# Twenty residual loads of a second output product: eight spread over SyncE's weight loads, twelve begun by ScalarE

## The chip, the cores and the metric

The kernel runs on one core of a Trainium2 chip. The metric is the device time of one execution in microseconds (us). The core's engines are TensorE (PE, matrix products), VectorE (DVE), ScalarE (ACT), GpSimd (POOL) and SyncE (SP), which here only begins transfers. Each works through its own instruction list in order and waits on semaphores for the others. Transfers between the main memory (HBM) and the on-chip memory (SBUF) are begun by SyncE, ScalarE or GpSimd and carried by 16 DMA engines.

## The reference

One layer over 128 context tokens and 512 noisy tokens, 1024 features each, all in float32:

```
x = x + 0.5 * gt1 * swiglu(norm(x) * (1 + sc1) + sh1, w_ffn1_in, w_ffn1_out)
x = x + gt2 * mixer(norm(x) * (1 + sc2) + sh2)          # convolution and gated DeltaNet heads
x = x + 0.5 * gt3 * swiglu(norm(x) * (1 + sc3) + sh3, w_ffn2_in, w_ffn2_out)
y = norm(x) * norm_final
...
def _swiglu(h, w_in, w_out):
    a, b = jnp.split(h @ w_in, 2, axis=-1)
    return (jax.nn.silu(a) * b) @ w_out
```

The change lies in the last product, `(silu(a) * b) @ w_ffn2_out` with 2816 hidden features, and in the residual `x` that is added to it.

## The kernel before

Float32 values are split into a high half (`_hi`, rounded to the format that TensorE takes at speed) and a low half (`_lo`, the rest), and each product is made of three matmuls: high by high, high by low, low by high. ScalarE makes the high halves, VectorE the low ones.

Until the second SwiGLU's input product the activations lie features by tokens. The second output product turns this round: the hidden activations `g` are the stationary operand and a row of weights is the moving one, 128 hidden features (partitions) by 512 output columns, so that the result lies tokens by features. The weights come as 84 such rows, numbered p. One row passes a line of stations:

- SyncE (`load_out_rows`, line 666) loads row p into `w_row`, a ring of eight buffers, from the weights `in_w_ffn_out` or from `d_ws`, a table of sums of weight blocks that GpSimd has written to HBM earlier. From row 8 on it waits until row p - 8 has its low half.
- ScalarE (`out_hi`, line 1884) makes `ring_hi` of it, a ring of four, and waits for TensorE to be done with row p - 4.
- VectorE (`out_lo`, line 2600) makes `ring_lo`.
- TensorE (`stripe`, line 1543) multiplies, in matmuls of 128x128 by 128x512.

Between the weight rows ScalarE and VectorE also make the halves of `g` (`g_hi`, line 1874, and `g_lo`, line 2593; tiles `gs_hi` and, in the plain rows, `gp_hi`).

The rows come in this order. Rows 0 to 31 are eight groups of four (`four`), six matmuls a row. Rows 32 to 55 are eight groups of three (`left`). Rows 56 to 61 are the six plain rows of the left half of the columns (`p_plain(0, r)`), for each of which TensorE makes five products of three matmuls. Rows 62 to 77 are eight groups of two (`right`), rows 78 to 83 the plain rows of the right half.

The residual comes back in this stage. Earlier VectorE has turned `x` in blocks of 32x32 into `xb`, and SyncE has stored it features by tokens in the HBM table `d_xb`. A residual load brings 32 tokens (partitions) by 1024 features into `yo`, as 32x32 runs of 32 numbers, 128 bytes each; 20 such loads, four for each of the five token tiles, bring all 640 tokens. VectorE waits for all of them at once, and for the two gate broadcasts `gb`, after it has made the low half of row 65:

```
for k in range(1, NH):
    for j in range(2):
        out_lo(p_right(k, j))
    if k == 1:
        dve.wait_ge(in_rows, 16 * (T // 32 + 2))
    if k > 1 and k - 2 < NC:
        residual_rows(0, k - 2)
```

`residual_rows` multiplies a result by the gate (`moved`) and adds it to `yo`. After the last row ScalarE and VectorE sum squares, normalise, and SyncE stores the outputs.

The kernel before has all 20 residual loads in SyncE's list, inside the loop over the weight rows (`load_out_rows`).

Of the kernel before, what the change touches and what calls it, by code (L numbers as in the profile page):

```python
# [36 lines left out]
P = 128  # L37
D = 1024
KD = D // P
TP, TS = 128, 512  # L40
T = TP + TS
TH = T // 2
NC = T // P
# [39 lines left out]
def p_four(k, j):  # L83
    return 4 * k + j
# [6 lines left out]
def p_right(k, j):  # L91
    return 7 * NH + NPL + 2 * k + j

def p_plain(c, r):
    return (7 + 2 * c) * NH + NPL * c + r

def w_block(p):

    if p < 4 * NH:
        k, j = divmod(p, 4)
        return ((k, 0, None), (k, 0, 1), (k, 0, 0), (k, 0, 2))[j]
    if p < 7 * NH:
        k, j = divmod(p - 4 * NH, 3)
        return ((k, 0, None), (NH + k, 0, None), (k, 0, 3))[j]
    if p < p_right(0, 0):
        return p - 5 * NH, 0, None
    n = p - p_right(0, 0)
    return (n // 2 + NH * (n % 2) if n < 2 * NH else n), 1, None  # L110
# [51 lines left out]
def hybrid_layer(nc, x_prompt, x_sample, state_f, state_b, c, c_ctx, w_ada, b_ada, norm1, w1i, w1o, norm_mix,  # L162
# [3 lines left out]
    with ctx:  # L166
# [3 lines left out]
        def sb(name, shape, dt, at=None):  # L170
            size = int(np.prod(shape[1:])) * (2 if dt == BF16 else 4)
            if at is None:
                at = place["at"]
                place["at"] += (size + 31) // 32 * 32
            return nc.alloc_sbuf_tensor_at(name, shape, dt, offset=at)
# [160 lines left out]
        def view(t, dims):  # L336

            return bass.AP(tensor=t.tensor, offset=t.offset, ap=dims)
# [13 lines left out]
        yo = sb("yo", [P, NC, D], F32, at=at_h + 12 * KB)  # L352
# [31 lines left out]
        d_xb = nc.dram_tensor("d_xb", [KD, P, T], F32).ap()  # L384
# [102 lines left out]
        xt_rdy, st_rows, in_rows = (sem(n) for n in ("xt_rdy", "st_rows", "in_rows"))  # L487
# [32 lines left out]
        def operand(p):  # L520

            return w_raws[p % 8], raw_in(p)

        PIECES = ((0, 0, TP, 0, 0), (0, TP, TH, 1, TP), (1, 0, TH, 1, TH))

# [49 lines left out]
        def _(sp):  # L576
# [75 lines left out]
            def load_out_rows():  # L652

                sp.wait_ge(st_rows, 16 * (GROUPS_DN + 2 + KD + 2))
                for i in range(2):
                    sp.wait_ge(ws_in[i], WS_IN)
                for n in range(R_ALL):
                    if n == 4:
                        sp.wait_ge(pr_done, LAST + 5)
                    if n == 6:  # L660
                        sp.wait_ge(*c12_rdy(SE[1] - 1))
                    if n >= 8:
                        sp.wait_ge(*lo_of(n - 8))
                    row, c, made = w_block(n)
                    src = w_out_v[1][:, row, OW * c:OW * c + OW] if made is None else d_ws[made, row]
                    sp.dma_start(w_raws[n % 8][:, :], src).then_inc(fr_in[n % 8], 16)
                    if n == 10:
                        sp.wait_ge(pr_done, 7 * SE[1])
                        sp.wait_ge(op_rdy, 7 * SE[1])
                        for j in range(2):  # L670
                            sp.dma_start(gb[:, j, :], d_gate[j:j + 1, :].to_broadcast([P, D])).then_inc(in_rows, 16)
                    if n >= 12 and n % 2 == 0 and (n - 12) // 2 < NC:
                        t = (n - 12) // 2
                        for b in range(4):
                            sp.dma_start(yo[32 * b:32 * b + 32, t, :].rearrange("p (c j) -> p c j", j=32),
                                         view(d_xb[0, 0, P * t + 32 * b:], [[T, 32], [32 * T, D // 32], [1, 32]])
                                         ).then_inc(in_rows, 16)
                    if n == p_right(3, 1):
                        sp.dma_start(nf_b[:, :], norm_f.rearrange("(a f) -> a f", a=1).to_broadcast([P, D])
                                     ).then_inc(nf_in, 16)  # L680
# [13 lines left out]
            def load_pairs(f):  # L694

                sp.wait_ge(mm_done, U_OUT[f])
                load_pair(f, S0[f] + 1, 1, pair_cols(NP[f] + 1))
                r0 = S0[f] // 2 + 1
                if f == 1:
                    for k in range(KD):  # L700
                        s = 2 * r0 + k
                        sp.wait_ge(op_rdy, 7 * s - 8)
                        load_pair(f, s, k % 2, pair_cols(NP[f] - S0[f] + s))
                        store_turned(k)
                    r0 += KD // 2
                with sp.Fori(r0, SE[f] // 2) as r:
                    for q in range(2):
                        sp.wait_ge(op_rdy, 14 * r + (7 * q - 8))
                        load_pair(f, None, q, lambda b: bass.ds(2 * P * r + (P * (NP[f] - S0[f] + q) + b * FF), P))
                sp.wait_ge(op_rdy, 7 * (SE[f] - 2) + 6)  # L710
                if f == 0:
                    load_out_columns(U_OUT[f], w_out_v[f])
                else:
                    load_out_rows()
# [938 lines left out]
        def _(act):  # L1653
# [195 lines left out]
            def g_hi(i):  # L1849

                if i < 2 * NH:
                    k = i // 2
                    act.wait_ge(pr_done, LAST + (2, 2, 3, 3, 3, 4, 4, 6)[k])
                    act.wait_ge(*s_made(k))
                    dst = gs_hi[:, k, 2 * (i % 2):2 * (i % 2) + 2, :].rearrange("p a t -> p (a t)")
                    src = g32[:, k, P:5 * P] if i % 2 == 0 else xs[:, k, :]
                elif i < 4 * NH:
                    k = i // 2 - NH
                    act.wait_ge(*mm_of(p_four(k, 3)))
                    if i % 2 == 0:  # L1860
                        dst, src = gs_hi[:, k, 0:2, :].rearrange("p a t -> p (a t)"), g32[:, NH + k, P:5 * P]
                    else:
                        dst = gs_hi[:, k, 3, :].rearrange("p (a t) -> p a t", a=2)
                        src = g32[:, k:k + NH + 1:NH, 0:P]
                elif i < 4 * NH + NPL:
                    r = i - 4 * NH
                    act.wait_ge(*mm_of(p_four(NH - 1, 3)))
                    act.wait_ge(*g_made(1, 2 * NH + r))
                    dst, src = gp_hi[:, r, :], g32[:, 2 * NH + r, :]
                else:  # L1870
                    b = i - 4 * NH - NPL
                    act.wait_ge(ps_rdy, PS + (8 if b == 0 else 15))
                    dst, src = gs_hi[:, 4 * b:4 * b + 4, 2, :], s4[b][:, :, :]
                nc.scalar.activation(dst, src, ACT.Copy).then_inc(gh_rdy, 1)

            def out_hi(p):

                src, ready = operand(p)
                act.wait_ge(*ready)
                if p > 3:  # L1880
                    act.wait_ge(*mm_of(p - 4))
                else:
                    act.wait_ge(pr_done, LAST + (1, 1, 6, 6)[p])
                nc.scalar.activation(ring_hi[p % 4][:, :], src[:, :], ACT.Copy).then_inc(fo_hi, 1)  # L1884
# [403 lines left out]
            for k in range(NH - 1):  # L2288
                p = p_four(k + 1, 0)
# [23 lines left out]
            for r in range(NPL):  # L2313
                g_hi(4 * NH + r)
                out_hi(p_plain(0, r))
            for b in range(2):
                out_hi(p_right(0, b))
                g_hi(4 * NH + NPL + b)
# [20 lines left out]
        def _(dve):  # L2339
# [423 lines left out]
            def residual(m, j, done, a_slot, n):  # L2763

                dve.wait_ge(mm_done, done)
                if j == 0:
                    dve.wait_ge(gain_rdy, 5 if m else 4)
                for bnk, b0, b1, i, t0 in PIECES:
                    last = nc.vector.scalar_tensor_tensor(
# [791 lines left out]
```

## Time and profile before

| | |
|---|---|
| median of 3 runs | 1294.96 us (1290.78 to 1295.73) |
| the profiled execution's own time | 1295.59 us |
| its span, first to last instruction | 1293.7 us |
| TensorE busy | 1264.2 us (98%) |
| VectorE, ScalarE, GpSimd busy | 983.6, 588.1, 141.5 us |
| second output product, row 0 to the first store | 1136.69 to 1282.72 us |

All times within the profiled execution count from the start of its span. The profile gives busy time, idle time and what ended it (the releaser) by engine, line and tile. TensorE's matmuls overlap in a pipeline: of two matmuls in a row, the distance between their starts is what one costs.

### The profile page before, as it was taken

How to read it: one execution, taken by the hardware profiler on the slowest of the kernel's cores; microseconds unless marked ns; L12 is line 12 of the kernel's file. 1: busy time of each engine (PE TensorE's matmuls, PEld its weight loads, DVE VectorE, ACT ScalarE, POOL GpSimd, SP SyncE). 2: the span in 40 equal slices, each digit the busy share in tenths (PEclk: the TensorE clock that was granted, in tenths of full speed). 3: DMA queues.
4: the chain of work that ended last, by engine and by line, in shares of the span. 5: the costliest groups of instructions: out<-in, count | busy, mean ns of one | idle time of the engine just before them, and what ended most of it. 6: DMA issues, size and time to landing. Idle time of an engine off the chain costs nothing.

```text
span 1293.7 us, 23360 instructions
## 1 busy us (share of the span) xinstructions
PE 1264.2 (98%) x8861; PEld 1211.0 (94%) x8861; DVE 983.6 (76%) x1646; ACT 588.1 (45%) x1002; POOL 141.5 (11%) x145
## 2 busy tenths in 40 slices
PE   8999999999999999999999999999999999988997
PEld 7889999999999999999999899999999999976886
DVE  5668877787887864666899867647988898867767
ACT  6514543345532225664333553436544343456643
POOL 0000222222000000003323663000000000000000
PEclk9999999999999999999999999999999999999999
DMA  9871767666576735348873552242243423287642
GB/s 371 295 270 31 190 153 191 156 163 166 163 215 194 220 107 142 99 119 190 260 211 64 154 149 83 66 88 60 66 128 96 143 71 97 65 212 233 191 139 90
DMA packets 250615, 197.31 MB, mean 153 GB/s; under 512 B 48321, under 2 KB 211622, under 8 KB 249254
## 3 DMA queue, kind: packets, MB, share of 16 engines
q1 hardware_dynamic: 241076, 176.00, 45.6%
q0 software_dynamic: 7840, 19.40, 7.5%
q8 instruction: 53, 0.87, 0.3%
q10 hardware_dynamic: 1618, 0.81, 0.2%
q14 instruction: 28, 0.23, 0.1%
HBM read 181.58 MB, written 36.61 MB: 169 GB/s over the span
## 4 chain that ended last, share of the span: by engine, by line
PE 74%; DVE 9%; DMA 6%; ACT 4%; issue 3%; POOL 2%; another core or an unknown queue 0%; SPq 0%; POOLq 0%; DVEq 0%; ACTq 0%
PE ps L1123 32%; PE ps L930 24%; PE ps L1543 8%; PE ps L1500 3%; DMA d_ex<-d_gc 2%; DMA w_row<-d_ws 2%; PE ps L1053 1%; DVE w_lo L2344 1%; DMA w_raw<-in_w_ffn_in 1%; PE ps L1486 1%; DVE cv L2831 1%; ACT w_hi L1659 1%; DVE sub_tmp L2951 1%; DVE pn L2413 1%; PE ps L998 1%
## 5 line engine op out<-in xcount | busy, mean ns | idle before, releaser
L1659 ACT ACTIVATE w_hi<-w_raw 128x1024 fp32r<-128x1024 f32 (+1 forms) x79 | 81.8, 1036 | 205.9 <-PE ps L930 163.8
L930 PE MATMUL ps<-h_hi,w_hi 128*128 128x320 f32 x736 | 171.9, 315 | 2.8 <-DVE w_lo L2344 2.7
L930 PE MATMUL ps<-h_lo,w_hi 128*128 128x320 f32 x736 | 169.5, 311 | 0.0
L930 PE MATMUL ps<-h_hi,w_lo 128*128 128x320 f32 x736 | 169.2, 311 | 0.0
L930 PEld LDWEIGHTS ps<-h_hi,w_hi 128*128 128x128 f32 x736 | 123.6, 189 | 7.5 <-issue 7.2
L2344 DVE TENSOR_TENSOR w_lo<-w_raw,w_hi 128x1024 fp32r<-128x1024 f32 (+1 forms) x79 | 100.0, 1267 | 37.2 <-ACT w_hi L1659 35.1
L1123 PE MATMUL ps<-T_hi,S_hi 128*128 128x320 f32 x408 | 126.0, 309 | 0.0
L1123 PE MATMUL ps<-T_hi,S_lo 128*128 128x320 f32 x408 | 126.0, 309 | 0.0
L1123 PE MATMUL ps<-T_lo,S_hi 128*128 128x320 f32 x408 | 125.9, 309 | 0.0
L930 PEld LDWEIGHTS ps<-h_hi,w_lo 128*128 128x128 f32 x736 | 124.6, 189 | 0.0
L930 PEld LDWEIGHTS ps<-h_lo,w_hi 128*128 128x128 f32 x736 | 124.3, 189 | 0.0
L2752 DVE SCALAR_TENSOR_TENSOR cw_acc<-cw_raw,silu_c,cw_acc 128x1024 f32<-128x1024 f32 x70 | 86.1, 1279 | 8.4 <-DMA cw_raw<-in_w_ada 5.7
L2600 DVE TENSOR_TENSOR ring_lo<-w_row,ring_hi 128x512 fp32r<-128x512 f32 x84 | 57.1, 688 | 42.6 <-ACT ring_hi L1884 41.3
L1123 PE MATMUL ps<-B_hi,A_hi 128*128 128x320 f32 x264 | 81.5, 309 | 0.5 <-issue 0.5
L1123 PE MATMUL ps<-B_lo,A_hi 128*128 128x320 f32 x264 | 81.4, 308 | 0.0
L1123 PE MATMUL ps<-B_hi,A_lo 128*128 128x320 f32 x264 | 81.4, 308 | 0.0
L1884 ACT ACTIVATE ring_hi<-w_row 128x512 fp32r<-128x512 f32 x84 | 52.4, 628 | 63.6 <-PE ps L1543 45.4
L930 PE MATMUL ps<-g_hi,w_hi 128*128 128x320 f32 x352 | 80.8, 311 | 0.2 <-DVE w_lo L2344 0.2
L930 PE MATMUL ps<-g_lo,w_hi 128*128 128x320 f32 x352 | 80.2, 309 | 0.0
L930 PE MATMUL ps<-g_hi,w_lo 128*128 128x320 f32 x352 | 80.2, 309 | 0.0
L1836 ACT ACTIVATE sa<-ps 128x320 f32<-128x320 f32 x34 | 14.9, 438 | 135.9 <-PE ps L1123 135.9
L1123 PEld LDWEIGHTS ps<-T_lo,S_hi 128*128 128x128 f32 x408 | 76.6, 188 | 0.0
(429 smaller groups left out, 3194.0 us busy)
## 6 DMA issues: line engine op xcount, KB each, us to landing
w_raw<-in_w_ffn_in SPq DMA_DIRECT2D x50, 512.0 KB, 4.8
cw_raw<-in_w_ada SPq DMA_DIRECT2D x40, 512.0 KB, 4.4
w_more<-in_w_ffn_in SPq DMA_DIRECT2D x34, 512.0 KB, 5.1
ada_w<-in_w_ada SPq DMA_DIRECT2D x16, 1024.0 KB, 9.0
w_raw<-in_w_mix_in SPq DMA_DIRECT2D x28, 512.0 KB, 4.4
w_row<-in_w_ffn_out SPq DMA_DIRECT2D x52, 256.0 KB, 3.0
d_ws<-in_w_ffn_out POOLq DMA_DIRECT2D x48, 256.0 KB, 5.3
w_row<-d_ws SPq DMA_DIRECT2D x32, 256.0 KB, 3.7
```

Source lines behind the costliest of these rows:

```text
L930: last = pe.matmul(to[a_slot][b], w, m[:, k0 + k, part[b]], start=start and k == 0 and n == 0, stop=stop and k == kt - 1 and n == 2)
L998: last = pe.matmul(adap[32 * g:32 * g + 32, 0:512], ccol[:, k, :], ada_w[:, n % ADA, g * 512:(g + 1) * 512], start=k == 0, stop=k == KD - 1)
L1053: pe.matmul(accw[s][b], w, m[:, k, PARTW[b]], start=k == 0 and n == 0, stop=k == KD - 1 and n == 2)
L1123: last = pe.matmul(to, a, m[:, k, :], start=not again and k == 0 and n == 0, stop=k == 3 and n == 2, skip_group_check=again)
L1500: last = pe.matmul(acc[s][b], w, m[:, k % 4, PART[b]], start=k == 0 and n == 0, stop=k == KD - 1 and n == 2)
L1543: last = pe.matmul(ps[bank][:, 0:f1 - f0], g, w, start=start and n == 0, stop=stop and n == 2, skip_group_check=True)
L1659: nc.scalar.activation(w_hi[:, slot, 0:kt * P], w_raw[:, slot, 0:kt * P], ACT.Copy).then_inc(hi_ready, 1)
L1836: nc.scalar.activation(c11, X, ACT.Silu).then_inc(act_ev, 1)
L1884: nc.scalar.activation(ring_hi[p % 4][:, :], src[:, :], ACT.Copy).then_inc(fo_hi, 1)
L2344: nc.vector.tensor_tensor(w_lo[:, slot, 0:kt * P], w_raw[:, slot, 0:kt * P], w_hi[:, slot, 0:kt * P].bitcast(F32), ALU.subtract).then_inc( ...
L2600: nc.vector.tensor_tensor(ring_lo[p % 4][:, :], operand(p)[0][:, :], ring_hi[p % 4][:, :].bitcast(F32), ALU.subtract).then_inc(fo_rdy, 1)
L2752: nc.vector.scalar_tensor_tensor(out=to[:, i, :], in0=raw_at(n)[:, :], scalar=silu_c[:, k, i:i + 1], in1=to[:, i, :], op0=ALU.mult, op1=AL ...
```

## The change

The four residual loads of a token tile stood together behind each of the weight loads 12, 14, 16, 18 and 20. Now a function `turned_rows(eng, i)` begins the i-th of the 20 loads on an engine of choice. SyncE begins loads 0 to 7, one behind each of the weight loads 12, 14, ..., 26. ScalarE begins loads 8 to 19, two behind the high half of each plain row 56 to 61. VectorE's wait for all 20 stays where it is.

```diff
+        def turned_rows(eng, i):
+
+            t, b = divmod(i, 4)
+            eng.dma_start(yo[32 * b:32 * b + 32, t, :].rearrange("p (c j) -> p c j", j=32),
+                          view(d_xb[0, 0, P * t + 32 * b:], [[T, 32], [32 * T, D // 32], [1, 32]])).then_inc(in_rows, 16)
+
...
-                    if n >= 12 and n % 2 == 0 and (n - 12) // 2 < NC:
-                        t = (n - 12) // 2
-                        for b in range(4):
-                            sp.dma_start(yo[32 * b:32 * b + 32, t, :].rearrange("p (c j) -> p c j", j=32),
-                                         view(d_xb[0, 0, P * t + 32 * b:], [[T, 32], [32 * T, D // 32], [1, 32]])
-                                         ).then_inc(in_rows, 16)
+                    if n >= 12 and n % 2 == 0 and (n - 12) // 2 < 4 * 2:
+                        turned_rows(sp, (n - 12) // 2)
...
             for r in range(NPL):
                 g_hi(4 * NH + r)
                 out_hi(p_plain(0, r))
+                for i in range(2):
+                    turned_rows(act, 8 + 2 * r + i)
```

In SyncE's list, from the gate broadcasts on, weight loads (`w_row_...`, one number for each of the eight ring buffers) and residual loads (`yo`) stood so before:

```order
L671 DMA gb<-d_gate 128x1024 x2
L666 DMA w_row_196<-d_ws 128x512
L666 DMA w_row_197<-in_w_ffn_out 128x512
L675 DMA yo<-d_xb 32x32x32 x4
L666 DMA w_row_198<-d_ws 128x512
L666 DMA w_row_199<-d_ws 128x512
L675 DMA yo<-d_xb 32x32x32 x4
L666 DMA w_row_200<-d_ws 128x512
L666 DMA w_row_193<-in_w_ffn_out 128x512
L675 DMA yo<-d_xb 32x32x32 x4
```

The same place of SyncE's list in the changed kernel, where line 527 is `turned_rows`:

```order
L677 DMA gb<-d_gate 128x1024 x2
L672 DMA w_row_196<-d_ws 128x512
L672 DMA w_row_197<-in_w_ffn_out 128x512
L527 DMA yo<-d_xb 32x32x32
L672 DMA w_row_198<-d_ws 128x512
L672 DMA w_row_199<-d_ws 128x512
L527 DMA yo<-d_xb 32x32x32
L672 DMA w_row_200<-d_ws 128x512
L672 DMA w_row_193<-in_w_ffn_out 128x512
L527 DMA yo<-d_xb 32x32x32
```

Three of four residual loads have gone from between the pairs of weight loads; the weight loads keep their order, and three more pairs have a residual load behind them than before.

In ScalarE's list, at the first plain rows, the high halves of `g` (`gp_hi`) and of the weight rows (`ring_hi`) stood so before:

```order
L1874 ACTIVATE gp_hi<-g_223 128x640
L1884 ACTIVATE ring_hi_201<-w_row_193 128x512
L1874 ACTIVATE gp_hi<-g_223 128x640
L1884 ACTIVATE ring_hi_202<-w_row_194 128x512
L1874 ACTIVATE gp_hi<-g_223 128x640
L1884 ACTIVATE ring_hi_203<-w_row_195 128x512
```

The same place of ScalarE's list in the changed kernel:

```order
L1876 ACTIVATE gp_hi<-g_223 128x640
L1886 ACTIVATE ring_hi_201<-w_row_193 128x512
L527 DMA yo<-d_xb 32x32x32 x2
L1876 ACTIVATE gp_hi<-g_223 128x640
L1886 ACTIVATE ring_hi_202<-w_row_194 128x512
L527 DMA yo<-d_xb 32x32x32 x2
L1876 ACTIVATE gp_hi<-g_223 128x640
L1886 ACTIVATE ring_hi_203<-w_row_195 128x512
L527 DMA yo<-d_xb 32x32x32 x2
```

Two residual loads now stand between the high half of a plain row and the halves behind it, six times over.

## Rows read from the trace of the kernel before

**Rows 1.** The page's busy us, share of the span, and instructions of TensorE.

```profile
PE 1264.2 (98%) x8861; PEld 1211.0 (94%) x8861; DVE 983.6 (76%) x1646; ACT 588.1 (45%) x1002; POOL 141.5 (11%) x145
```

**Rows 2.** Who waited for whom, 1110 to 1293: us in total, times, longest.

```profile
ACT ring_hi L1884 <- DMA w_row<-d_ws: 15.6, 8, 3.5
...
PE ps L1543 <- DVE ring_lo L2600: 7.5, 7, 1.8
```

**Rows 3.** TensorE's timeline: start, duration (us), line, operation, [idle before it].

```profile
1136.69 0.40 PE L1543 MATMUL ps<-ring_hi,gs_hi 128*128 128x512 f32 x1
...
1153.21 0.39 PE L1543 MATMUL ps<-ring_hi,gs_hi 128*128 128x512 f32 x1
...
1173.91 0.51 PE L1543 MATMUL ps<-ring_hi,gs_hi 128*128 128x512 f32 x1 [1.70 <-DVE ring_lo L2600]
```

**Rows 4.** Second output's line by stretch: length, busy us (count) on PE and PEld, PEclk, DMA.

```profile
1136.60:1173.80 37.20, 30.29 (x126) 23.14 (x126) 1.00 0.93 231
1136.60:1153.10 16.50, 16.41 (x72) 13.57 (x73) 1.00 0.83 242
```

**Rows 5.** SyncE's timeline: start, us to issue the run, transfers in it.

```profile
1142.06 7.51 SPq L675 DMA_DIRECT2D yo<-d_xb  x4
...
1150.69 3.91 SPq L675 DMA_DIRECT2D yo<-d_xb  x4
...
1155.83 3.55 SPq L675 DMA_DIRECT2D yo<-d_xb  x4
...
1160.60 3.63 SPq L675 DMA_DIRECT2D yo<-d_xb  x4
...
1165.40 3.55 SPq L675 DMA_DIRECT2D yo<-d_xb  x4
```

**Rows 6.** Busy us by engine in stretches, then PEclk, DMA share, GB/s.

```profile
1155.00:1160.00 5.00, 3.39 (x14) 2.50 (x15) 2.33 (x4) 1.73 (x4) 0.00 (x0) 1.00 1.08 221
1175.00:1180.00 5.00, 5.00 (x24) 4.11 (x23) 4.69 (x9) 3.79 (x8) 0.00 (x0) 1.00 1.00 375
1210.00:1220.00 10.00, 10.00 (x46) 8.29 (x45) 6.43 (x11) 6.26 (x12) 0.00 (x0) 1.00 0.65 199
1220.00:1230.00 10.00, 10.00 (x45) 8.13 (x44) 6.91 (x11) 5.45 (x9) 0.00 (x0) 1.00 0.50 150
1230.00:1240.00 10.00, 10.00 (x45) 8.04 (x44) 4.34 (x5) 3.79 (x5) 0.00 (x0) 1.00 0.36 121
```

**Rows 7.** The chain that ended last, 1100 to 1294: start, us, what.

```profile
1140.62 7.62 DMA w_row<-d_ws
...
1195.06 82.31 PE ps L1543 x357
```

**Rows 8.** The residual's tile, 1138 to 1172: ns to issue one, us to landing.

```profile
L675 SPq DMA_DIRECT2D yo<-d_xb x20: 303/566/3592, 1142.1 to 1168.6; - x20
...
DMA to landing us min/median/max: 2.7/4.0/7.8
```

**Rows 9.** ScalarE's timeline at the first plain rows (56, 57, 61).

```profile
1219.25 0.63 ACT L1884 ACTIVATE ring_hi<-w_row 128x512 fp32r<-128x512 f32 x1
...
1220.42 0.61 ACT L1884 ACTIVATE ring_hi<-w_row 128x512 fp32r<-128x512 f32 x1
...
1230.35 0.63 ACT L1884 ACTIVATE ring_hi<-w_row 128x512 fp32r<-128x512 f32 x1 [2.24 <-PE ps L1543]
```

**Rows 10.** TensorE's timeline where rows 56 and 57 begin.

```profile
1223.08 0.40 PE L1543 MATMUL ps<-ring_hi,gp_hi 128*128 128x512 f32 x1
...
1226.59 0.40 PE L1543 MATMUL ps<-ring_hi,gp_hi 128*128 128x512 f32 x1
```

**Rows 11.** VectorE's timeline at rows 64, and 65 with 66.

```profile
1241.51 0.69 DVE L2600 TENSOR_TENSOR ring_lo<-w_row,ring_hi 128x512 fp32r<-128x512 f32 x1 [1.32 <-ACT ring_hi L1884]
1245.01 1.46 DVE L2600 TENSOR_TENSOR ring_lo<-w_row,ring_hi 128x512 fp32r<-128x512 f32 x2 [2.81 <-ACT ring_hi L1884]
```

**Rows 12.** A transfer begun by ScalarE earlier in the program.

```profile
690.01 0.62 ACTq L2070 DMA_DIRECT2D d_sel<-sub_x  x1
```

## Prediction

> **What bounds the kernel now.** I read the busy shares first. TensorE is busy for 98% of a 1293.7 us span [rows 1], so only a stretch in which it stands still has time to give, or one that makes it stand still. The change touches the second output stage alone (from 1136.7 us on), so I read next who waits for whom there. TensorE's matmuls stood idle 7.5 us in 7 waits for `ring_lo`, VectorE's low half of a weight row, and ScalarE's `ring_hi` waited 15.6 us for 8 weight loads from `d_ws` [rows 2]. So weight rows land late, and through ScalarE and VectorE TensorE waits for them.
>
> Third, the size of the loss, from starts of matmuls instead of idle times, since a matmul after a stall also runs slower at first. Row 0 starts at 1136.69; 72 matmuls (12 rows of six) later it is 1153.21, so one takes (1153.21 - 1136.69) / 72 = 0.2294 us and a row 1.376 us [rows 3]. Ahead of the matmul at 1173.91 stand 126 matmuls [rows 4], or 21 rows. They should take 126 x 0.2294 = 28.9 us; they took 37.2. **TensorE loses 8.3 us here.** It falls ahead of rows 13 to 21, since the first 72 matmuls show no idle time beyond 0.1 us (16.41 of 16.50 us busy) [rows 4].
>
> Fourth, why they are late. SyncE's queue shows four residual loads in one piece after every second weight load: 7.51 us for the first four, then 3.91, 3.55 and 3.63 [rows 5]. From block to block it is 5.14, 4.77 and then 4.80 us to the fifth at 1165.40 [rows 5], for two weight rows that TensorE uses up in 2.75. The 16 DMA engines are full then: share 1.08 at 221 GB/s, where weights alone get 375 GB/s at share 1.00 [rows 6]. A weight load of 262,144 bytes so costs 0.70 us of all engines, and a residual load (4.79 - 2 x 0.70) / 4 = **0.85 us**, for half the bytes. Residuals hold up weights by filling the engines in front of them; that SyncE is held while it issues is the same backlog seen from the queue.
>
> **The change, part by part.** No matmul, byte or VectorE instruction is added or removed. What moves is 20 residual loads.
>
> *Eight stay on SyncE, one behind each second weight load.* Each pair of rows then asks for 1.40 + 0.85 = 2.25 us of the engines, under the 2.75 us in which TensorE uses it. So the supply is faster than the demand, if row 13 is in time. The load of row 11, issued at 1140.62, landed 7.62 us later, at 1148.2 [rows 7], behind the two gate broadcasts. Behind it now come row 12 (0.70), one residual (0.85) and row 13 (0.70): 1150.5. TensorE wants row 13 at 1136.69 + 13 x 1.376 = 1154.6, and the two halves take 0.63 and 0.69 ahead of that [rows 9, 11], so it must land by 1153.2. There are 2.7 us in hand, and each pair adds 0.5. So I count the full 8.3 us as gained. The lower bound takes the residual at its dearest, 7.51 / 4 = 1.88 us [rows 5]: a pair then asks 3.28 us, 0.53 too much, over eight pairs 4.2 us. Less the 2.7 in hand, 1.5 is lost and 6.8 gained; with nothing in hand, 4.1. I take 0.85 because the last two intervals between blocks give it, and the one before gives 0.94; the first block stood behind the gate broadcasts.
>
> *Twelve go to ScalarE, two behind each `ring_hi` of the six plain rows.* ScalarE is in order, so each pair holds up the next `gp_hi` and `ring_hi`, VectorE's `ring_lo` behind them, and then TensorE. ScalarE's `ring_hi` of row 56 starts at 1219.25 and that of row 57 at 1220.42: 1.17 us a row without the loads [rows 9]. TensorE begins row 56 at 1223.08 and row 57 at 1226.59: 3.51 us a row [rows 10]. With an issue of x us, the low half of row 56 + r is ready 2.51 + r (2.34 - 2x) us ahead of TensorE (2.51 is 1223.08 less 1219.25, 0.63 and 0.69; 2.34 is 3.51 less 1.17). For row 62, the first behind all twelve, that is 16.55 - 12x: no stall up to x = 1.38. ScalarE has issued no residual so far. Its nearest row, a small store, took 0.62 us [rows 12]; on SyncE a residual took 0.30 at least, 0.57 in the middle, 3.59 at most [rows 8], and 0.89 (3.55 / 4) in a full queue [rows 5]. I take at most 0.89, because the plain rows have free engines: **nothing** on the path. The upper end is 3.59: row 62 would be 26.5 us late.
>
> *The engines there.* Twelve loads take 12 x 0.85 = 10.2 us. From 1210 to 1240 the DMA share is 0.65, 0.50 and 0.36 [rows 6], so 3.5 + 5.0 + 6.4 = 14.9 us are free. Weight loads run eight rows, some 28 us, ahead. Cost nothing; without that cover, up to 10.2 us.
>
> *VectorE's wait for all residuals moves from long satisfied to near.* It stands behind the low half of row 65, whose pair with row 66 begins at 1245.01, so at 1245.6 [rows 11]. Queued behind it are the low halves of rows 66 on and the first residual sums. ScalarE reaches row 61 at 1230.35, held by TensorE and not by its loads [rows 9]; two issues of 0.89 end at 1232.8, and the slowest landing was 7.8 us [rows 8]: 1240.6. That is 5.0 us in time; the likely landing of 4.0 us leaves 8.8.
>
> *Behind the stage.* TensorE's next piece on the chain runs 82.31 us, from 1195.06 [rows 7], with VectorE's and ScalarE's tail behind it. Nothing there waits for a transfer that the stalls had given time to, so 8.3 us go through. 
>
> **The rivals.** *Half stays* (gain 4.1, 1290.9): residuals cost 1.88 us each and row 13 has nothing in hand. For it speaks the first block; against it the three that follow. *The stalls are the weights' own* (no change, 1295): every long wait is for `d_ws` rows, which might land late whatever stands before them. Against it: at 1175 the same rows come at 375 GB/s and TensorE is busy 5.00 of 5.00 us [rows 6].
>
> *The work only moves* (1296.9 at worst): the engines' work is conserved, and the twelve loads hold up weights among the plain rows for all of their 10.2 us, which eats the 8.3. Against it stand the 14.9 us free and the eight rows of lead. The Trainium skill speaks for this rival ("DMA: Bandwidth & Descriptors", "Issuing engines are not separate DMA queues"): loads begun by ScalarE and SyncE run on the same 16 engines, and a second issuer saves only its sequencer's time. By that rule the move to ScalarE gives nothing by itself; the trace agrees in that the engines, not SyncE, are full, and what is left as a gain is the later hour.
>
> *ScalarE becomes the wait* (slower): at x over 1.38 us row 62 is late. The loss is 12x - 16.55, so it decides at x = 2.07, where 8.3 us are eaten; at 3.59 the sum is 1294.96 - 8.3 + 26.5 = 1313.2. For it: SyncE did take 3.59 once. Against: that was behind the gate broadcasts, on full engines.
>
> **How the numbers follow.** Chances: forecast 0.66, half stays 0.09, weights' own 0.10, work only moves 0.07, ScalarE 0.08. A measurement of this kernel tells about 0.5%, 6.5 us. The forecast's own spread (6.8 to 8.3, and some noise of a median of runs that lie 5 us apart) falls beyond that in nine of ten: 0.60 faster, and 0.01 from the other cases. ScalarE's case is over 6.5 us slower from x = 2.61 on, most of it as its rows are either near 0.9 or near 3.6: 0.06. The rest, 0.33, is the same. The range goes from 1284 (the forecast less 2.7 of noise) to 1292.5, which takes in half stays and leaves out no change and slower: about 0.8. The forecast alone: 1284 to 1289.5.
>
> **What would show it.** In the changed profile, matmul 126 of the stage should start some 29 us after row 0, not 37; `ring_hi`'s waits for `d_ws` should be nearly gone; two weight rows and a residual should pass SyncE every 2.75 us; ScalarE should issue each residual in under 1 us; `ring_lo` of row 62 should not be waited for; VectorE should go from row 65's low half to row 66's without a wait for a DMA. Wrong would be: stalls of rows 13 to 20 that stay, an issue above 1.4 us on ScalarE, or a wait for `yo` at row 65.

## The result, and the profile of the changed kernel

The changed kernel takes 1287.94 us (median of 19 runs, 1283.78 to 1291.91), the kernel before 1296.75 (19 runs beside them, 1290.78 to 1302.33). The ratio is 0.9933, with a 95% interval of 0.9920 to 0.9946: 8.7 us less (1296.75 x 0.0067). The forecast was 8.3 us less, taken from a median of three runs of the kernel before, 1294.96; beside the changed kernel its median was 1.8 us higher.

Of the two profiled executions the spans are 1293.7 and 1286.7 us, 7.0 apart. That is less than the gain of the stage itself, because row 0 of the second output product starts at 1138.13 instead of 1136.69: the work ahead of the stage took 1.4 us longer in this execution. Over all profiles below row 0 starts anywhere from 1133.82 to 1141.11, in no order that follows from the edits. So the stage is best measured from its own first matmul. From row 0 to the last matmul start of the line it took 1286.92 - 1136.69 = 150.23 us before and 1279.92 - 1138.13 = 141.79 us after: **8.44 us less**. The last matmul before, and after:

```profile
1286.92 0.28 PE L1543 MATMUL ps<-ring_lo,gp_hi 128*128 128x256 f32 x1
```

```profile
1279.92 0.28 PE L1545 MATMUL ps<-ring_lo,gp_hi 128*128 128x256 f32 x1
```

From that start to the end of the span it is 6.8 us in both, and in every kernel below.

First, TensorE's timeline of the changed kernel (start, duration, line, operation) at row 0 and 126 matmuls later, and under it, as in [rows 4], the busy time and count of that line between the two:

```profile
1138.13 0.40 PE L1545 MATMUL ps<-ring_hi,gs_hi 128*128 128x512 f32 x1
...
1167.00 0.40 PE L1545 MATMUL ps<-ring_hi,gs_hi 128*128 128x512 f32 x1
```

```profile
1138.05:1166.95 28.90, 28.82 (x126) 23.79 (x127) 1.00 1.00 264
```

The same 126 matmuls now take 1167.00 - 1138.13 = 28.87 us instead of 37.22, and 28.82 of 28.90 us are busy. No stall is left ahead of rows 13 to 21. The waits of the whole stretch say the same (who waited for whom: us in total, times, longest; compare [rows 2]):

```profile
ACT ring_hi L1886 <- DMA w_row<-d_ws: 2.1, 1, 2.1
...
PE ps L1545 <- DVE ring_lo L2604: 0.6, 2, 0.4
```

ScalarE's waits for `d_ws` fell from 15.6 us to one of 2.1 us, TensorE's for `ring_lo` from 7.5 us to 0.6. The chain that ended last (start, us, what) has no transfer of a weight row in this stage any more:

```profile
1138.29 44.79 PE ps L1545 x195
...
1188.04 82.33 PE ps L1545 x357
```

Next SyncE's queue (start, us to issue, transfers), to be read beside [rows 5]: the first, the fourth and the last of its eight residual loads. Between the residual loads there are always two weight loads:

```profile
1143.50 0.74 SPq L527 DMA_DIRECT2D yo<-d_xb  x1
...
1154.47 0.43 SPq L527 DMA_DIRECT2D yo<-d_xb  x1
...
1163.37 0.43 SPq L527 DMA_DIRECT2D yo<-d_xb  x1
```

From the fourth to the eighth it is (1163.37 - 1154.47) / 4 = 2.23 us for two weight loads and a residual, while SyncE fills its ring of eight faster than TensorE empties it. The forecast's sum for the engines was 2.25.

ScalarE's part, at the plain rows: its activations and, marked ACTq, its issues of residual loads:

```profile
1212.25 0.63 ACT L1886 ACTIVATE ring_hi<-w_row 128x512 fp32r<-128x512 f32 x1
1212.27 0.99 ACTq L527 DMA_DIRECT2D yo<-d_xb  x2
1213.36 0.74 ACT L1876 ACTIVATE gp_hi<-g 128x640 fp32r<-128x640 f32 x1 [0.47 <-PE ps L1545]
1213.46 1.40 ACTq L527 DMA_DIRECT2D yo<-d_xb  x1
1214.00 0.62 ACT L1886 ACTIVATE ring_hi<-w_row 128x512 fp32r<-128x512 f32 x1
...
1224.21 0.62 ACT L1886 ACTIVATE ring_hi<-w_row 128x512 fp32r<-128x512 f32 x1
```

The twelve issues add up to 11.9 us, 0.99 each, more than the 0.89 that I took at most. Five of the twelve took 1.40 us or more, 1.52 the longest, and an issue above 1.4 us on ScalarE was one of the forecast's signs of being wrong; why it cost nothing stands below. The DMA engines were busier there than I had it (busy us by engine, PEclk, DMA share, GB/s; compare [rows 6]):

```profile
1155.00:1160.00 5.00, 5.00 (x24) 4.11 (x23) 4.45 (x8) 3.95 (x8) 0.00 (x0) 1.00 1.10 268
1210.00:1220.00 10.00, 10.00 (x45) 8.21 (x44) 6.47 (x10) 5.68 (x9) 0.00 (x0) 1.00 0.95 210
1220.00:1230.00 10.00, 10.00 (x44) 8.04 (x44) 4.86 (x7) 4.10 (x6) 0.00 (x0) 1.00 1.07 232
```

TensorE is busy in all of it. The last lines to check are VectorE's at rows 65 and 66, behind which its wait for all 20 residual loads stands, and the residual's own (ns to issue, us to landing):

```profile
1238.01 1.46 DVE L2604 TENSOR_TENSOR ring_lo<-w_row,ring_hi 128x512 fp32r<-128x512 f32 x2 [2.81 <-ACT ring_hi L1886]
```

```profile
L527 ACTq DMA_DIRECT2D yo<-d_xb x12: 367/1050/1515, 1212.3 to 1224.1; - x12
...
DMA to landing us min/median/max: 3.5/5.0/6.1
```

VectorE's two low halves run as one piece, so the wait between them cost nothing. The last issue began at 1224.1 and no landing took over 6.1 us: all residuals were there by 1230.2, 8.4 us before VectorE asked.

### The profile page after: what moved, and what is told of

The parts are those of the page before. It is cut to its first block, busy times and chain, and to the rows that moved or that the text cites. A ratio compares the mean times of both kernels' runs of the same rounds, so it can differ in the third digit from the quotient of the medians.

```text
span 1286.7 us, 23360 instructions
## 1 busy us (share of the span) xinstructions
PE 1262.6 (98%) x8861; PEld 1210.9 (94%) x8861; DVE 983.5 (76%) x1646; ACT 588.5 (46%) x1002; POOL 141.6 (11%) x145
## 4 chain that ended last, share of the span: by engine, by line
PE 77%; DVE 9%; DMA 4%; ACT 3%; issue 3%; POOL 2%; another core or an unknown queue 1%; SPq 0%; POOLq 0%; DVEq 0%; ACTq 0%
PE ps L1125 33%; PE ps L932 24%; PE ps L1545 10%; PE ps L1502 3%; DMA d_ex<-d_gc 2%; PE ps L1055 1%; DVE w_lo L2348 1%; DMA w_raw<-in_w_ffn_in 1%; PE ps L1488 1%; DVE cv L2835 1%; ACT w_hi L1661 1%; DVE sub_tmp L2955 1%; DVE pn L2417 1%; PE ps L1000 1%; POOL Rc L3472 1%
## 5 line engine op out<-in xcount | busy, mean ns | idle before, releaser
L1838 ACT ACTIVATE sa<-ps 128x320 f32<-128x320 f32 x34 | 14.9, 438 | 136.5 <-PE ps L1125 136.5
L1125 PEld LDWEIGHTS ps<-T_hi,S_hi 128*128 128x128 f32 x408 | 76.6, 188 | 0.0
```

The costliest lines, as they stand in the source:

```text
L1125: last = pe.matmul(to, a, m[:, k, :], start=not again and k == 0 and n == 0, stop=k == 3 and n == 2, skip_group_check=again)
L1838: nc.scalar.activation(c11, X, ACT.Silu).then_inc(act_ev, 1)
```

## The experiments

My theory is the one of the forecast: what delayed the weight rows was the time of the 16 DMA engines, 0.70 us for a weight load and 0.85 for a residual load, against 2.75 us in which TensorE uses two rows. Rivals: SyncE's list, held while it issues; the move to ScalarE; blocks of four as such; and rows of the table of sums that are late by themselves.

Every ratio below is to the kernel before, run beside the experiment: 1296.75 us beside the changed kernel, 1295.99 beside the next four, 1295.75 beside the last three, with 7 to 12 runs of each experiment. The stage counts from row 0 to the last matmul start, as above, in one profiled execution of each kernel; the four kernels near 141.8 us agree within 0.03 us.

| kernel | median, us | ratio (95%) | stage, us | against changed |
|---|---|---|---|---|
| before | 1296.75, 1295.99, 1295.75 | 1 | 150.23 | +8.44 |
| changed | 1287.94 | 0.9933 (0.9920 to 0.9946) | 141.79 | 0 |
| all 20 on SyncE | 1288.23 | 0.9941 (0.9922 to 0.9961) | 141.77 | -0.02 |
| blocks of four apart | 1287.21 | 0.9945 (0.9924 to 0.9966) | 141.76 | -0.03 |
| blocks among left rows | 1293.15 | 0.9972 (0.9953 to 0.9991) | 144.44 | +2.65 |
| ScalarE in one burst | 1294.15 | 0.9989 (0.9972 to 1.0005) | 148.84 | +7.05 |
| two a pair | 1293.74 | 0.9981 (0.9963 to 0.9998) | 147.30 | +5.51 |
| twelve by SyncE, same hour | 1287.82 | 0.9937 (0.9917 to 0.9957) | 141.77 | -0.02 |
| blocks by GpSimd | 1294.97 | 0.9997 (0.9978 to 1.0015) | 146.88 | +5.09 |

The ratios alone do not tell the burst and the blocks by GpSimd from the kernel before: their intervals include 1. Blocks among the left rows stand 5.8 us under before by the stage and 3.6 by the ratio; blocks by GpSimd 3.4 and 0.4. Behind the stage nothing differs, so the difference lies ahead of it or is noise; its cause stays open, and the readings below go by the stage.

**All 20 on SyncE.** Is it ScalarE that carries the gain? Here ScalarE begins none.

```diff
-                    if n >= 12 and n % 2 == 0 and (n - 12) // 2 < 4 * 2:
+                    if n >= 12 and n % 2 == 0 and (n - 12) // 2 < 4 * NC:
                         turned_rows(sp, (n - 12) // 2)
...
-                for i in range(2):
-                    turned_rows(act, 8 + 2 * r + i)
```

> All 20 residual loads on SyncE, one behind every second weight load (12, 14, ..., 50); ScalarE begins none. Theory (the 16 DMA engines: a pair of weight rows asks 1.40 + 0.85 = 2.25 us of them and TensorE takes 2.75): no stall, as fast as the changed kernel, 8 to 9 us under before (ratio 0.993). Rival (the move of twelve loads to ScalarE carries the gain): twelve twentieths of it are lost again, 3 to 4 us under before.

The stage takes 141.77 us, as in the changed kernel, and the ratios agree within their intervals. The move to ScalarE is not needed for the gain; the spreading is.

**Twelve by SyncE, at the same hour.** The twelve late loads stay at the hour of the plain rows, but SyncE begins them.

```diff
+                    if p_plain(0, 0) + 8 <= n < p_plain(0, NPL) + 8:
+                        for i in range(2):
+                            turned_rows(sp, 8 + 2 * (n - p_plain(0, 0) - 8) + i)
...
-                for i in range(2):
-                    turned_rows(act, 8 + 2 * r + i)
```

> As the changed kernel, but the twelve late loads are begun by SyncE, two behind each of the weight loads 64 to 69, which run at the hour of the plain rows. Theory (engines; it matters when a load runs, not who begins it): as the changed kernel within 1 us, 8 to 9 us under before. Rival (the second issuer matters): SyncE is held about 1 us a load and the weight rows come late, 2 us or more slower than the changed kernel.

Again 141.77 us. Who begins a load makes no difference here.

**Blocks by GpSimd.** The counter-test: the old hour and the old blocks, with SyncE's list free of residuals.

```diff
-                    if n >= 12 and n % 2 == 0 and (n - 12) // 2 < 4 * 2:
-                        turned_rows(sp, (n - 12) // 2)
...
-                for i in range(2):
-                    turned_rows(act, 8 + 2 * r + i)
...
-                    dve.wait_ge(in_rows, 16 * (T // 32 + 2))
+                    dve.wait_ge(in_rows, 16 * 2)
+                    dve.wait_ge(in_pool, 16 * (T // 32))
...
+            for t in range(NC):
+                pool.wait_ge(*lo_of(4 + 2 * t))
+                for b in range(4):
+                    turned_rows(pool, 4 * t + b, in_pool)
```

The residual loads count on a semaphore of their own here, `in_pool`, and VectorE waits for it at the old place.

> All 20 begun by GpSimd, in blocks of four let go when the low halves of rows 4, 6, 8, 10 and 12 are made, the hour of the blocks in the kernel before; SyncE begins weight rows only. Theory (engines full): weight rows late again ahead of rows 13 to 21, 5 us of stall or more, within 4 us of before, unless GpSimd itself spreads the loads out. Rival (SyncE's list was the trouble, not the engines): no stall, 8 to 9 us under before.

The stage lost 5.1 us to the changed kernel. TensorE's timeline shows the longest stalls, ahead of rows 13 to 15 ([idle before <- releaser]), and the windows the full engines (busy us by engine, PEclk, DMA share, GB/s):

```profile
1160.37 0.50 PE L1544 MATMUL ps<-ring_hi,gs_hi 128*128 128x512 f32 x1 [0.77 <-DVE ring_lo L2601]
...
1163.26 0.50 PE L1544 MATMUL ps<-ring_hi,gs_hi 128*128 128x512 f32 x1 [1.23 <-DVE ring_lo L2601]
...
1166.05 0.50 PE L1544 MATMUL ps<-ring_hi,gs_hi 128*128 128x512 f32 x1 [1.14 <-DVE ring_lo L2601]
```

```profile
1155.00:1160.00 5.00, 4.45 (x19) 3.02 (x17) 1.16 (x3) 1.67 (x3) 3.53 (x5) 1.00 1.06 237
1160.00:1165.00 5.00, 3.31 (x12) 2.10 (x12) 2.21 (x4) 1.62 (x4) 0.00 (x0) 1.00 1.04 230
```

SyncE was not held by a residual here, and the rows were late all the same. It began the load of row 13 at 1146.71, as the first of three, and ScalarE, which waited for it, took the row up at 1158.96:

```profile
1146.71 2.73 SPq L673 DMA_DIRECT2D w_row<-d_ws  x3
```

```profile
1158.96 0.63 ACT L1885 ACTIVATE ring_hi<-w_row 128x512 fp32r<-128x512 f32 x1 [1.79 <-DMA w_row<-d_ws]
```

That is 5.6 and 17.85 us after row 0. In the kernel with blocks among the left rows (below), where no residual is begun yet, SyncE begins the same load at 5.6 us too, and ScalarE takes the row up at 14.04 without waiting for it. So the rival of SyncE's list falls. The loss is smaller than before. GpSimd did not keep to blocks of four: it issued fifteen one behind the other, one every 0.78 us, stopped for 9.8 us and issued the last five:

```profile
1146.73 11.80 POOL L527 DMA_DIRECT2D yo<-d_xb  x15 [355.38 <-DVE ring_lo L2601]
1168.31 3.88 POOL L527 DMA_DIRECT2D yo<-d_xb  x5 [9.79 <-issue]
```

By the medians this kernel stands no better than before, though its stage is 3.4 us shorter; its row 0 started latest of all, at 1141.11, and whether GpSimd's wait or chance did that stays open.

**Blocks of four apart.** Is it the block?

```diff
-                    if n >= 12 and n % 2 == 0 and (n - 12) // 2 < 4 * 2:
-                        turned_rows(sp, (n - 12) // 2)
+                    if n >= 12 and (n - 12) % 8 == 0 and (n - 12) // 8 < NC:
+                        for i in range(4):
+                            turned_rows(sp, (n - 12) // 2 + i)
...
-                for i in range(2):
-                    turned_rows(act, 8 + 2 * r + i)
```

> The blocks of four of the kernel before, all on SyncE, but behind every eighth weight load (12, 20, ..., 44) instead of every second. Theory (engines, mean load): four pairs ask 4 x 1.40 + 3.4 = 9.0 us of 11.0, a block of 3.4 us meets 2.7 us in hand or more: at most 1 us of stall, 7.5 to 8.5 us under before. Rival (a block of four is in itself what stalls): five blocks at 2.0 us each, about as before (within 2 us).

The blocks did no harm: 141.76 us. ScalarE did wait for weight rows, and TensorE only for two short waits of 0.6 us together (us in total, times, longest):

```profile
ACT ring_hi L1887 <- DMA w_row<-d_ws: 10.0, 6, 2.8
...
PE ps L1546 <- DVE ring_lo L2603: 0.6, 2, 0.4
```

Ten us of waiting, up to 2.8 us at a time, stayed inside ScalarE's lead over TensorE. By the ratio this kernel is 7.1 us under before (4.4 to 9.8), by the stage 8.5, as forecast. A block does no harm if the lead covers it and the mean load leaves time to win the lead back.

**Blocks among the left rows.** Is it the table of sums? The five old blocks, at the old density, now among rows two thirds of which come from the weights themselves.

```diff
-                    if n >= 12 and n % 2 == 0 and (n - 12) // 2 < 4 * 2:
-                        turned_rows(sp, (n - 12) // 2)
+                    if n >= 34 and n % 2 == 0 and (n - 34) // 2 < NC:
+                        for i in range(4):
+                            turned_rows(sp, 2 * (n - 34) + i)
```

> The same five blocks of four behind every second weight load, but behind loads 34, 36, ..., 42, which are mostly rows of the weights themselves and only one in three from the table of sums; nothing but weights stands in rows 12 to 31. Theory (engines): five blocks ask 4.8 us for each pair that TensorE takes in 2.75, 10.2 us in all, less 3 to 7 us in hand since the gate broadcasts are long over: stalls of 3 to 7 us, 1.5 to 6 us under before. Rival (the rows of the table of sums are late by themselves): the stalls stay ahead of rows 13 to 21, about as before; rival (neither): no stall in the second place, 8 to 9 us under before.

Matmul 126 starts 28.87 us after row 0: with nothing but weights in rows 12 to 31, the stalls ahead of rows 13 to 21 are gone, although the rows from the table are the same. New stalls stand where the blocks are (TensorE's timeline):

```profile
1197.28 0.50 PE L1546 MATMUL ps<-ring_hi,gs_hi 128*128 128x512 f32 x1 [0.48 <-DVE ring_lo L2603]
...
1198.59 0.50 PE L1546 MATMUL ps<-ring_hi,gs_hi 128*128 128x512 f32 x1 [0.35 <-DVE ring_lo L2603]
...
1201.82 0.50 PE L1546 MATMUL ps<-ring_hi,gs_hi 128*128 128x512 f32 x1 [0.90 <-DVE ring_lo L2603]
```

So the rows from the table were not late by themselves. The price is 2.65 us, just under the 3 that I gave as the least: with the gate broadcasts out of the way there was more in hand. The load of row 34, the last one ahead of the blocks, landed 36.4 us after row 0, and TensorE takes that row at 47.3, 1.3 of which the two halves need: 9.6 us in hand, where I had 3 to 7.

**Two a pair.** Where is the threshold?

```diff
-                    if n >= 12 and n % 2 == 0 and (n - 12) // 2 < 4 * 2:
-                        turned_rows(sp, (n - 12) // 2)
+                    if n >= 12 and n % 2 == 0 and (n - 12) // 2 < 2 * NC:
+                        for i in range(2):
+                            turned_rows(sp, n - 12 + i)
```

> All 20 on SyncE, two behind each second weight load (12, 14, ..., 30). Theory (engines): a pair asks 1.40 + 1.70 = 3.10 us, 0.35 over TensorE's 2.75; ten pairs 3.5 us, less 2.7 in hand: a stall of about 1 us, 6 to 8.5 us under before. Rival (any residual load between the pairs costs in proportion to their number): two against four a pair, 4 us under before.

The rate was right and the loss was not. SyncE's queue, second and last pair:

```profile
1151.33 1.04 SPq L527 DMA_DIRECT2D yo<-d_xb  x2
...
1175.99 1.05 SPq L527 DMA_DIRECT2D yo<-d_xb  x2
```

Eight pairs apart, (1175.99 - 1151.33) / 8 = 3.08 us for SyncE to issue a pair of rows with its residuals, against 3.10 expected, and 0.33 over TensorE's 2.75. But the stage lost 5.51 us and not 1. Stalls ahead of rows 23 to 31 (the distances of starts beyond 0.23 us, added up) are 2.6 us. ScalarE's timeline at rows 13 and 31, which it takes up as soon as they have landed, tells why:

```profile
1152.61 0.63 ACT L1887 ACTIVATE ring_hi<-w_row 128x512 fp32r<-128x512 f32 x1 [1.16 <-DMA w_row<-d_ws]
...
1182.05 0.63 ACT L1887 ACTIVATE ring_hi<-w_row 128x512 fp32r<-128x512 f32 x1 [1.89 <-DMA w_row<-d_ws]
```

Over these nine pairs the rows landed (1182.05 - 1152.61) / 9 = 3.27 us apart, more than the 3.08 at which SyncE issued them and 0.52 over TensorE's 2.75: 4.7 us in all. Row 13 came 14.45 us after row 0, 2.1 us before it had to, and 4.7 less 2.1 is the 2.6 lost. More came behind row 31, where TensorE waited for `U`, a sum that VectorE makes after four low halves of `g` and one of a row, all queued behind row 31's low half:

```profile
1187.29 0.77 PE L1546 MATMUL ps<-ring_hi,gs_hi 128*128 128x512 f32 x1 [2.17 <-DVE U L3324]
1187.85 0.63 PE L1546 MATMUL ps<-ring_hi,g_lo 128*128 128x512 f32 x1
```

```profile
1186.00:1187.00 1.00, 0.00 (x0) 0.00 (x0) 1.00 (x2) 1.00 (x3) 0.00 (x0) 1.00 1.04 399
1187.00:1188.00 1.00, 0.71 (x2) 0.65 (x3) 1.00 (x3) 0.89 (x2) 0.00 (x0) 0.63 0.84 313
1188.00:1189.00 1.00, 1.00 (x4) 0.77 (x3) 1.00 (x3) 0.00 (x0) 0.00 (x0) 0.50 0.64 225
...
1191.00:1192.00 1.00, 1.00 (x6) 0.82 (x5) 1.00 (x3) 0.06 (x1) 0.00 (x0) 1.00 0.49 168
```

Together this is 2.6 + 2.3 + 1.7 = 6.6 us; the changed kernel has 1.1 us of waits for `ring_lo` at rows 32 and 35 that this one does not have, which leaves the 5.5. By the ratio the kernel stands 2.5 us under before, nearer the rival's 4 than the theory's 6 to 8.5. The rival falls all the same: one residual a pair, all 20 of them, cost nothing above, where in proportion it would have cost a quarter of the 8.4.

**ScalarE in one burst.** What does an issue cost where it does lie on the path?

```diff
-                for i in range(2):
-                    turned_rows(act, 8 + 2 * r + i)
+                if r == 0:
+                    for i in range(12):
+                        turned_rows(act, 8 + i)
```

> As the changed kernel, but ScalarE issues all twelve loads in one go behind the high half of row 56. Theory (ScalarE in order, 12 issues of about 1.0 us each against 2.51 + 2.34 = 4.85 us in hand at row 57): low half of row 57 is 5 to 7.5 us late, TensorE waits that long, 1 to 4 us under before. Rival (what ScalarE issues is hidden whatever its order): 8 to 9 us under before.

ScalarE's timeline and TensorE's behind it:

```profile
1211.75 0.63 ACT L1886 ACTIVATE ring_hi<-w_row 128x512 fp32r<-128x512 f32 x1
1211.77 10.33 ACTq L527 DMA_DIRECT2D yo<-d_xb  x12
1222.19 0.74 ACT L1876 ACTIVATE gp_hi<-g 128x640 fp32r<-128x640 f32 x1 [9.81 <-issue]
```

```profile
1218.85 0.40 PE L1545 MATMUL ps<-ring_lo,gp_hi 128*128 128x512 f32 x1
1224.44 0.80 PE L1545 MATMUL ps<-ring_hi,gp_hi 128*128 128x512 f32 x1 [5.19 <-DVE ring_lo L2605]
```

Twelve issues took 10.33 us, 0.86 each, which is the engines' price of a residual load: ScalarE was held at the pace at which the engines drained. With x = 0.86 the forecast's formula makes row 57 late by 12 x 0.86 - 4.85 = 5.5 us; TensorE started it 1224.44 - 1218.85 - 0.23 = 5.4 us late. ScalarE's issues are free in the changed kernel only because they are spread over six rows. The stage lost 7.05 us in all, 1.7 more than the wait: the granted clock fell to 0.50 during the wait and stood at 0.98 again in the stretch from 1228, 3.6 us after TensorE had gone on at 1224.44.

## Why the prediction was right

*What bounds the stage.* Right: TensorE lost 8.3 us ahead of rows 13 to 21 for want of weight rows, and all of it came back, 8.44 us by the stage and 8.7 by the ratio (7.0 to 10.4).

*Why the rows were late.* Shown: full DMA engines. It does not matter who begins the loads (all on SyncE, twelve at the same hour) nor whether they come in blocks (blocks apart); it stays when SyncE is freed of them (GpSimd), and goes where the loads go (left rows). The Trainium skill's rule ("DMA: Bandwidth & Descriptors", "Issuing engines are not separate DMA queues") holds here: 141.77 us with SyncE alone, 141.79 with ScalarE. The rival for which it spoke, that the work only moves, fell: among the plain rows the engines were full, share 0.95 and 1.07, and the weights' lead of eight rows covered it. What in a residual load's 0.85 us is the engines' own time and what they wait for memory, no run separates.

*The price of a residual load.* Right to a tenth: 0.85 us was forecast; two a pair gives (3.08 - 1.40) / 2 = 0.84 by SyncE's issues and (3.27 - 1.40) / 2 = 0.94 by the rows' landing, the burst 0.86. The dearest case, 1.88 an issue, was no price but the time that SyncE was held: with blocks apart it was held 7.09 us by the third block too, long after the gate broadcasts, and nothing was lost.

*What is in hand at row 13.* Right in kind, not sized by one number. In the changed kernel ScalarE took row 13 up as soon as it had landed, 15.3 us after row 0:

```profile
1153.47 0.63 ACT L1886 ACTIVATE ring_hi<-w_row 128x512 fp32r<-128x512 f32 x1 [2.06 <-DMA w_row<-d_ws]
```

The forecast had the landing at 13.8 and the latest time at 16.5, so in this execution 1.2 us were in hand, not 2.7. Three other kernels have the same loads up to there: in twelve by SyncE and in the burst ScalarE got the row at 14.4 us, with 2.1 in hand, and with all 20 on SyncE it did not wait for it at all. It stayed above nothing each time, so no stall came of it. It is not what made two a pair miss its expectation: with two residuals ahead row 13 left 2.1 us there. That miss lies in the rate, 3.27 us a pair where 3.10 was expected, and in what followed at row 32, which the expectation did not have.

*ScalarE's issues.* The answer was right, two terms were not. An issue took 0.99 us and not 0.89. The sign of being wrong, one issue above 1.4 us, was too strict: by the forecast's own formula it is the mean that counts, and it stalls from 1.38 on. On the other side, issue and activations overlapped, which the formula puts one behind the other: `ring_hi` went from 1212.25 to 1224.21 over rows 56 to 61, 2.39 us a row, where 1.17 + 2 x 0.99 would be 3.15. Row 61's low half was ready at 1225.8, 7.8 us before TensorE began that row at 1233.6; by the formula it is 2.51 + 5 x 2.34 - 10 x 0.99 = 4.3 us, so the answer did not hang on the overlap.

*The engines among the plain rows.* The cover held; the free time was counted too widely. I set 10.2 us of loads against 14.9 us free over 30 us, but ScalarE begins all twelve within 12 us (1212.27 to 1224.13), so the engines were full there, share 0.95 and 1.07. TensorE's 10.00 busy of 10.00 us in both windows shows that the lead covered it.

*VectorE's wait.* Right: 8.4 us in time, 5.0 to 8.8 forecast.

*Behind the stage.* Right: TensorE's last piece on the chain is 82.33 us against 82.31, and the 6.8 us behind the last matmul start are the same, so nothing was given back.

## What to carry to other kernels

When a prefetch ring runs late, add up the DMA engines' time per step, small-run transfers at their own price (here 128 KB in runs of 128 bytes cost more than 256 KB of weights), and compare it with the time in which the consumer uses a step. What is over is lost once the lead is used up, whoever begins the transfers; spread the surplus over steps that have time left, and leave blocks alone where the mean fits and the lead covers one. Take the rate from when the data land, not from when they are issued: in two a pair the two were 3.27 and 3.08 us. Measure such a stage from its own first instruction, since in the profiles its start varied by 7.3 us, nearly the gain.

## What the runs showed of the hardware that was not expected

A stall of TensorE costs more than its length once the clock falls. In the kernel before, stalls of 1.6 to 1.8 us, some 5 us apart, left the granted clock at 1.00 [rows 4]. In the burst it fell while TensorE stood still for 5.19 us, and was at 0.50 until 1228, with TensorE at work again from 1224.44 (busy us by engine, PEclk, DMA share, GB/s):

```profile
1220.00:1221.00 1.00, 0.00 (x0) 0.00 (x0) 0.00 (x0) 0.00 (x0) 0.00 (x0) 1.00 0.96 151
1221.00:1222.00 1.00, 0.00 (x0) 0.00 (x0) 0.00 (x0) 0.00 (x0) 0.00 (x0) 0.61 1.12 175
1222.00:1223.00 1.00, 0.00 (x0) 0.00 (x0) 0.04 (x1) 0.81 (x2) 0.00 (x0) 0.50 1.12 175
...
1227.00:1228.00 1.00, 1.00 (x3) 0.74 (x3) 1.00 (x3) 0.52 (x1) 0.00 (x0) 0.50 0.62 213
1228.00:1229.00 1.00, 1.00 (x6) 0.81 (x5) 1.00 (x2) 0.00 (x0) 0.00 (x0) 0.98 0.83 254
```

